# A fused decoder layer: the gated MLP in three phases, its down projection by a seven-product scheme

## The reference, cut to what matters

```python
u = rmsnorm(h, ln_ffn)
g_up, v_up = jnp.split(u @ w_up, 2, axis=-1)          # w_up: 1024 x 6144
g_up = causal_dwconv(g_up, ffn_conv_w, ffn_conv_b)    # 3 taps along the tokens
h = h + (jax.nn.gelu(g_up) * v_up) @ w_down           # w_down: 3072 x 1024
gate = jax.nn.sigmoid(rmsnorm(h, ln_ple) @ w_ple_gate)
h = h + gate * (p @ w_ple_proj)
```

## Time and profile before

| what | value |
|---|---|
| median of three runs | 646.7 us |
| profiled execution, its span | 644.5 us |
| TensorE matmul, busy | 640.1 us, 99% |
| TensorE weight load, busy | 531.3 us, 82% |
| VectorE, ScalarE, GpSimd busy | 353.6, 297.8, 325.0 us |
| HBM read | 62.74 MB, 101 GB/s over the span |

### The profile page before, as it was taken

The page is one execution under the profiler, slowest core; times in us unless marked ns, Lnnn a source line. Parts: engine busy times, 40 slices in busy tenths (PEclk is TensorE's granted clock), DMA queues, the critical chain, the costliest instruction groups (busy, mean ns, idle before and its releaser), DMA issues.

```text
span 644.5 us, 8549 instructions
## 1 busy us (share of the span) xinstructions
PE 640.1 (99%) x2925; PEld 531.3 (82%) x2925; DVE 353.6 (55%) x503; ACT 297.8 (46%) x453; POOL 325.0 (50%) x240
## 2 busy tenths in 40 slices
PE   9999999999999999999999999999999999999997
PEld 7887788888888888888888888888888888888886
DVE  4682499978659777655555555555422222222734
ACT  6779944788745454333333333333322222224420
POOL 6673443642326557555555555555555555545430
PEclk9999999999999999999999999999999999999999
DMA  8652225640403333323222232222322222222201
GB/s 314 261 159 87 85 94 139 158 120 1 165 5 127 99 98 131 98 98 98 98 98 98 98 98 97 92 92 94 106 91 94 93 96 95 97 96 99 98 34 65
DMA packets 21480, 68.69 MB, mean 107 GB/s; under 512 B 2512, under 2 KB 3152, under 8 KB 21456
## 3 DMA queue, kind: packets, MB, share of 16 engines
q1 hardware_dynamic: 21168, 68.12, 32.0%
q10 hardware_dynamic: 288, 0.27, 0.1%
HBM read 62.74 MB, written 2.10 MB: 101 GB/s over the span
## 4 chain that ended last, share of the span: by engine, by line
PE 99%; DMA 1%; DVE 0%; issue 0%
PE bank L1151 30%; PE bank L1152 30%; PE bank L1153 30%; PE bank L1347 2%; PE bank L1333 1%; PE bank L1293 1%; PE bank L1197 1%; PE bank L1200 1%; PE bank L1205 1%; DMA lead<-in_lead_in 1%; PE bank L1263 1%; PE bank L1248 0%; PE bank L1314 0%; PE bank L1190 0%; PE bank L1290 0%; DVE fin L1122 0%
## 5 line engine op out<-in xcount | busy, mean ns | idle before, releaser
L383 POOL TENSOR_TENSOR wlo<-raw,whi 128x512 fp32r<-128x512 f32 x106 | 142.7, 1346 | 260.5 <-ACT whi L444 260.1
L444 ACT ACTIVATE whi<-raw 128x1024 fp32r<-128x1024 f32 x102 | 107.5, 1057 | 213.4 <-PE bank L1153 212.8
L1151 PE MATMUL bank<-uhi,whi 128*128 128x512 f32 x488 | 189.8, 389 | 0.0
L1152 PE MATMUL bank<-ulo,whi 128*128 128x512 f32 x488 | 189.8, 389 | 0.0
L1153 PE MATMUL bank<-uhi,wlo 128*128 128x512 f32 x488 | 189.8, 389 | 0.0
L384 POOL TENSOR_TENSOR wlo<-raw,whi 128x512 fp32r<-128x512 f32 x106 | 163.1, 1539 | 0.0
L1151 PEld LDWEIGHTS bank<-uhi,whi 128*128 128x128 f32 x488 | 91.6, 188 | 19.2
L1152 PEld LDWEIGHTS bank<-ulo,whi 128*128 128x128 f32 x488 | 91.6, 188 | 19.1
L1153 PEld LDWEIGHTS bank<-uhi,wlo 128*128 128x128 f32 x488 | 91.6, 188 | 18.8
L1069 DVE SCALAR_TENSOR_TENSOR tmp<-tmp,vec 128x511 f32<-128x511 f32 (+1 forms) x48 | 64.7, 1347 | 27.7 <-ACT tmp L690 24.7
L1151 PE MATMUL bank<-acthi,whi 128*128 128x512 f32 x192 | 74.7, 389 | 0.0
(11 more groups left out here) (215 smaller groups left out, 806.0 us busy)
## 6 DMA issues: line engine op xcount, KB each, us to landing
raw<-in_weights SPq DMA_DIRECT2D x106, 512.0 KB, 3.3
res<-in_x_t SPq DMA_DIRECT2D x8, 256.0 KB, 5.6
xtok<-in_x SPq DMA_DIRECT2D x4, 512.0 KB, 8.7
raw<-in_weights SPq DMA_DIRECT2D x7, 256.0 KB, 6.6
out<-fin SPq DMA_DIRECT2D x7, 256.0 KB, 2.0
k_more<-kT SPq DMA_DIRECT2D x6, 256.0 KB, 4.9
kT<-kT SPq DMA_DIRECT2D x3, 256.0 KB, 4.2
ptok<-in_p_t SPq DMA_DIRECT2D x1, 512.0 KB, 3.4
```

The source lines that it names most:

```text
L383: nc.gpsimd.tensor_tensor(wlo[s][:, 0:CW // 2], raw[s][:, 0:CW // 2], whi[s][:, 0:CW // 2].bitcast(F32), ALU.subtract)
L444: nc.scalar.activation(whi[s][:, :], raw[s][:, :], ACT.Copy).then_inc(w_hi, 1)
L1151: mm(o, ahi, bhi, start=start, stop=False)
L1152: mm(o, ahi, blo, start=False, stop=False)
```

## The change

The hidden channels are worked through in three phases. Each phase makes 8 channel tiles (4 pairs, 16 up chunks) and at once their share of the down projection (8 down chunks), which is added to `res`. So weight chunks come in the order 16 up, 8 down, three times; `acthi` and `actlo` go and the loops over chunks are written out.

The down projection is done by Strassen's scheme on blocks of two channel tiles (a pair) x two output tiles x two token halves of 256. For each pair VectorE makes five sums of the four quarters of the activations (`pair_sums`, 1280 columns in three instructions), ScalarE the high parts (`act_pair`), VectorE the low parts (`low_plain`, `low_sums`). A down chunk holds the four quarters of a weight block as 4 x 256 columns. Of its sums, two and two are VectorE's (`weight_sums_1`, `weight_sums_2`) and one is GpSimd's (`first_sum`); ScalarE makes the high parts, 512 + 512 + 768 columns (`down_high`); GpSimd subtracts for two of the low parts (`down_low`). For the three sums in `xhi` ScalarE writes -xhi into `xlo`, and a DMA issued from GpSimd, with `accum_op=ALU.add`, adds the sums `ws` to it, 384 KB. TensorE multiplies seven products, each in a half bank of 256 columns (`down`), two chunks to each of the four output pairs. For each output pair and phase VectorE adds the four banks to `res` in six dependent instructions (`combine`).

In the last phase the norm of the last block is tied to the combines (`norm_ple`, `finish_ple`), and `p` is loaded later, into the place of two of the `ws` buffers.

```diff
-C_DN = C_UP + 2 * FT
-C_PP = C_DN + 3 * KD
+PHASES = 3
+PH_CHUNKS = 2 * FT // PHASES + KD
+PH_PAIRS = FT // PHASES // 2
+C_PP = C_UP + PHASES * PH_CHUNKS
+DOWN = [(0, 0), (1, 0), (0, 1), (1, 1), (2, 0), (2, 1), (3, 0), (3, 1)]
+B11, B22, T6, T7, T4, T3, T1 = range(7)
...
+        SETS = ((0, 1, 3, 4), (5, 6, 7, 2))
...
+                elif isinstance(c, int) and down_index(c - RING) is not None:
+                    sp.wait_ge(d_lo, 2 * (down_index(c - RING) + 1))
+                    sp.wait_ge(w_sum, 2 * (down_index(c - RING) + 1))
...
+            for c in range(C_UP, N_CHUNKS):
                 load(c, c % RING)
+                if c == C_PP + 1:
+                    sp.wait_ge(act_lo, 2 * PHASES * PH_PAIRS)
+                    sp.dma_start(ptok[:, :, :], p_t[:, :, :]).then_inc(p_in, 16)
...
+            def first_sum(n):
+                c = down_chunk(n)
+                s, quarter = c % RING, raw[c % RING][:, :].rearrange("p (b w) -> p b w", w=HALF)
+                pool.wait_ge(raw_in[s], 16 * (c // RING))
+                if n >= RING:
+                    pool.wait_ge(x_low[n % RING], 16 * (n // RING))
+                nc.gpsimd.tensor_tensor(ws[n % RING][:, 4, :], quarter[:, 2, :], quarter[:, 3, :], ALU.add).then_inc(s1_ok, 1)
...
+                pool.wait_ge(d_hi, 4 * n + 4)
+                pool.dma_start(xlo[s][:, :], ws[n % RING][:, 2:5, :].rearrange("p b w -> p (b w)"), accum_op=ALU.add).then_inc(x_low[s], 16)
...
+            def act_pair(pair):
+                act.wait_ge(f_prod, 2 * pair + 2)
+                act.wait_ge(chunk_done, C_UP + pair // PH_PAIRS * PH_CHUNKS)
+                nc.scalar.activation(ahi[:, pair % PH_PAIRS, 0:2, :], yq[:, 0:4:3, :], ACT.Copy).then_inc(act_hi, 1)
+                act.wait_ge(t_ok, 3 * (pair + 1))
+                nc.scalar.activation(ahi[:, pair % PH_PAIRS, 2:7, :], ts[:, :, :], ACT.Copy).then_inc(act_hi, 1)
+            def down_high(n):
...
+                act.wait_ge(chunk_done, c - (RING - 1))
+                nc.scalar.activation(whi[s][:, 0:CW // 2], raw[s][:, CW // 2:CW], ACT.Copy).then_inc(d_hi, 1)
+                act.wait_ge(w_sum, 2 * n + 1)
+                nc.scalar.activation(whi[s][:, CW // 2:CW], sums[:, 0:2 * HALF], ACT.Copy).then_inc(d_hi, 1)
...
+                nc.scalar.activation(xhi[s][:, :], sums[:, 2 * HALF:5 * HALF], ACT.Copy).then_inc(d_hi, 1)
+                act.wait_ge(d_hi, 4 * n + 3)
+                nc.scalar.activation(xlo[s][:, :], xhi[s][:, :].bitcast(F32), ACT.Copy, scale=-1.0).then_inc(d_hi, 1)
...
+            def norm_ple(j):
+                act.wait_ge(d_step, 6 * (4 * (PHASES - 1) + j + 1))
+                for m in (2 * j, 2 * j + 1):
+                    nc.scalar.activation(uhi[:, m, :], res[:, m, :], ACT.Copy,
+                                         scale=vec[:, V_LN_PLE + m:V_LN_PLE + m + 1]).then_inc(u_hi, 1)
+                    act.wait_ge(acc_ok, KD + m - 1)
+                    nc.scalar.activation(tmp[:, 2 + m % 2, :], res[:, m, :], ACT.Square).then_inc(sqr, 1)
...
+                for i in range(KD):
+                    high(down_chunk(ph * KD + i) + RING)
+                    if ph == PHASES - 1:
+                        if i == 3:
+                            norm_ple(0)
+                        elif i == 4:
+                            norm_ple(1)
...
+                        elif i == 6:
+                            norm_ple(2)
+                        elif i == 7:
+                            norm_ple(3)
...
+                    up_product(f + 1)
+                    pair_sums(pair)
+                    low_plain(pair)
+                weight_sums_1(n0 + 4)
+                low_sums(pair)
+                weight_sums_2(n0 + 4)
...
+                combine(4 * ph)
+                weight_sums_1(n0 + 6)
+                weight_sums_2(n0 + 6)
+                combine(4 * ph + 1)
+                weight_sums_1(n0 + 7)
+                weight_sums_2(n0 + 7)
+                if ph < PHASES - 1:
+                    combine(4 * ph + 2)
+                    combine(4 * ph + 3)
+            finish_ple(0)
+            combine(4 * ph + 2)
+            finish_ple(1)
+            dve.wait_ge(x_low[1], 16 * 2 * PHASES)
             for k in range(2):
                 dve.wait_ge(p_hi, k + 1)
                 V.tensor_tensor(pTlo[:, k, :], ptok[:, k, :], pThi[:, k, :].bitcast(F32), ALU.subtract).then_inc(p_lo, 1)
+            combine(4 * ph + 3)
+            finish_ple(2)
+            finish_ple(3)
...
+            def down(n):
+                ph, i = divmod(n, KD)
+                j, h = DOWN[i]
+                s = down_chunk(n) % RING
+                if h == 0 and j < 2:
+                    pe.wait_ge(g_out, 8 * ph + 6 + 2 * j)
+                    pe.wait_ge(v_out, 8 * ph + 6 + 2 * j)
+                elif h == 0:
+                    pe.wait_ge(d_step, 6 * (4 * ph + j - 1))
+                b0, b1, b2, b3 = SETS[j % 2]
+                products = ((2 * b2, whi, wlo, 3, T7), (2 * b2 + 1, whi, wlo, 2, T6), (2 * b0 + 1, whi, wlo, 0, T3),
+                            (2 * b1 + 1, whi, wlo, 1, T4), (2 * b0, xhi, xlo, 5, B22), (2 * b1, xhi, xlo, 4, B11),
+                            (2 * b3, xhi, xlo, 6, T1))
+                pe.wait_ge(d_lo, 2 * (n + 1))
+                pe.wait_ge(act_lo, 2 * (PH_PAIRS * ph + 2 * h + 2))
+                for at_, high, low, q, x in products:
+                    if q == 5:
+                        pe.wait_ge(x_low[s], 16 * (n // RING + 1))
+                    for k in range(2):
...
+                        last = three(cell[:, at_, :], high[s][:, w], low[s][:, w], ahi[:, 2 * h + k, x, :], alo[:, 2 * h + k, x, :],
+                                     first, h == 1 and k == 1, True)
+                last.then_inc(chunk_done, 1)
```

More of the change, by code:

```diff
@@ new lines, in _ @@
+            for ph in range(PHASES):
+                for p in range(PH_PAIRS):
+                    pair = ph * PH_PAIRS + p
+                    f, c = 2 * pair, up_chunk(2 * pair, 0)
+                    if pair:
+                        high(c + RING)
+                    tap_up(f)
+                    if pair:
+                        high(c + RING + 1)
+                    gelu_up(f)
+                    high(c + RING + (2 if pair else 3))
+                    tap_up(f + 1)
+                    if pair and p < PH_PAIRS - 1:
+                        high(c + RING + 3)
+                    gelu_up(f + 1)
+                    if p == PH_PAIRS - 1:
+                        high(c + RING + 3)
+                    act_pair(pair)
+                for i in range(KD):
+                    high(down_chunk(ph * KD + i) + RING)
[4 more added lines that the diff above has]
+                            norm_ple(1)
+                        elif i == 5:
+                            act.wait_ge(p_in, 16)
+                            act.wait_ge(x_low[0], 16 * 2 * PHASES)
+                            act.wait_ge(d_lo, 2 * (PHASES * KD - 3))
+                            for k in range(2):
+                                nc.scalar.activation(pThi[:, k, :], ptok[:, k, :], ACT.Copy).then_inc(p_hi, 1)
+                        elif i == 6:
+                            norm_ple(2)
+                        elif i == 7:
+                            norm_ple(3)
@@ new lines, in up_product, with pair_sums @@
+            def up_product(f):
+                g, y = tmp[:, f % 2, :], tmp[:, 2 + f % 2, :]
+                dve.wait_ge(v_out, f + 1)
+                dve.wait_ge(f_gelu, f + 1)
+                V.tensor_tensor(y, g, y, ALU.mult).then_inc(f_prod, 1)
+            def pair_sums(pair):
+                dve.wait_ge(f_prod, 2 * pair + 2)
+                if pair:
+                    dve.wait_ge(act_lo, 2 * pair)
+                V.tensor_tensor(ts[:, 0:2, :], yq[:, 0:4:2, :], yq[:, 1:4:2, :], ALU.add).then_inc(t_ok, 1)
+                V.tensor_tensor(ts[:, 2:4, :], yq[:, 0:2, :], yq[:, 2:4, :], ALU.subtract).then_inc(t_ok, 1)
+                V.tensor_tensor(ts[:, 4, :], yq[:, 0, :], yq[:, 3, :], ALU.add).then_inc(t_ok, 1)
@@ new lines, in finish_ple @@
+            def finish_ple(j):
+                for m in (2 * j, 2 * j + 1):
+                    dve.wait_ge(u_hi, 2 * KD + m + 1)
+                    V.scalar_tensor_tensor(ulo[:, m, :], res[:, m, :], vec[:, V_LN_PLE + m:V_LN_PLE + m + 1],
+                                           uhi[:, m, :].bitcast(F32), ALU.mult, ALU.subtract).then_inc(u_lo, 1)
+                    dve.wait_ge(sqr, KD + m + 1)
+                    dve.wait_ge(acc_ok, KD + m)
+                    V.tensor_tensor(acc[:, :], acc[:, :], tmp[:, 2 + m % 2, :], ALU.add).then_inc(acc_ok, 1)
@@ L1438, in _, with up_pair @@
                 channels(C_UP + 4 + s, s, mbank[4 + s][:, :], uhi, ulo, 0, KD, True, True)
-            with pe.Fori(2, FT // 2) as it:
+            def up_pair(pair):
+                ph, p = divmod(pair, PH_PAIRS)
                 for t in range(2):
                     for half in range(2):
```

(21 more changed lines are left out.)

277 lines of the change are left out of this document (175 added, 102 removed).

## The result

The changed kernel takes 658.5 us (657.9 to 658.8) against 647.1 us (646.3 to 648.9): a ratio of 1.0168, 95% interval 1.0146 to 1.0190. It is slower by 11.4 us where 4.8 us less was forecast, and lies outside the range of 637.5 to 651.0.

A forecast was written before the change was run, and what follows sets the result against it. TensorE was taken to bound the kernel: -10.5 us of matmuls, +5.0 tail, +0.6 combine cover and +0.1 end of the up part make -4.8, so 641.9 us, range 637.5 to 651.

The forecast's parts named there:

- What bounds the kernel: Whole kernel: TensorE, busy 640.1 of 644.5 us, so only matmul time or a new TensorE stall moves the end.
- The matmul term: Down projection: 1008 matmuls of 256 columns at 119.1 ns replace 576 at 226.7 ns, 10.5 us less.
- the estimate of 14: Down projection: the saving in us if matmul steps followed the skill page's stated gap, 215.8 and 109.2 ns.
- The combine's cover of 0.4 us: Down part: combine(0) ends at 19.6, TensorE needs its banks at 20.0; 0.2 us per phase taken, 0.6 in all.
- The adding transfer: Down chunks: GpSimd's DMA lands 6 us after issue, about 1 on GpSimd; costs nothing below 9.7 us.
- The fourth rival: Down chunks: the adding transfer delays TensorE's fifth product; slower than before from 11.3 us on, 654.8 at 14; chance 0.13.
- The end of the up part: VectorE's chain behind the last up matmul takes 7 to 9.5 us of 10.0; 0.1 us taken, bounds 0 to 12.
- The contention: Up part: VectorE and GpSimd together fill 21.2 of 21.8 us per pair of channel tiles, nearly full but enough.
- The tail: Last phase: TensorE waits for pTlo, then pp, behind the combines and norms; 5.0 us of stall, bounds 3.3 to 9.
- the third: Rival, end of the up part: VectorE late by 1 to 4 us in each phase, 645 to 654; chance 0.22.

The follow-up runs named there:

- e1_order: Changed kernel with only the order at each up part's end altered: last pair's taps and sums first on ScalarE and VectorE; 661.2 us, ratio 1.0221.
- e9_order_tail: e7_apart_order_tail without any of GpSimd's waits for its own instructions, so the reorderings and the moved channel sum alone; 657.9 us, ratio 1.0171.
- e4_pool_lows: Changed kernel with the adding transfer undone: GpSimd subtracts all five low parts of a down chunk itself; 673.2 us, ratio 1.0411.
- e11_one_pause: e7_apart_order_tail with only one of GpSimd's waits for itself kept, behind the first sum after each adding transfer's issue; 641.5 us, ratio 0.9908.
- e13_small_transfer: e4_pool_lows plus an unused 8 KB transfer issued by GpSimd behind each subtraction of the three sums; 676.7 us.
- e2_tail: Changed kernel with only the tail reordered: pTlo ahead of finish_ple(1) on VectorE, keep_pp ahead of norm_ple(3) on ScalarE; 661.5 us, ratio 1.0232.
- e6_apart_order: Changed kernel with the order of e1_order and GpSimd waiting for the end of each of its own MLP instructions; 649.3 us, ratio 1.0033.
- e7_apart_order_tail: e6_apart_order plus the tail order of e2_tail, with the channel sum moved from the second gate chunk to the third; 645.0 us, ratio 0.9964.

## Why the prediction was wrong

- **What bounds the kernel**: right. All but 0.7 us of the result is TensorE's matmuls, its waits, its clock or the late start.
- **The matmul term** (119.1 ns, -10.5): right. Measured 120.0, -9.6; the estimate of 14 from the Trainium skill (TensorE: Matmul & The Clock Gate, Back-to-back issue gap) was not reached.
- **The combine's cover of 0.4 us** (+0.6): harmless in the kernel after, with no wait there, but it is where e1_order and e9_order_tail lost 4.3 to 5.4 us in each phase.
- **The adding transfer** (6 us to landing, about 1 on GpSimd, hidden below 9.7): right as a price, 5.8 and 0.9. The fourth rival did not occur. That its issue would change VectorE's turns was in no term.
- **The end of the up part** ("Cover 0.5 to 3 us", taken at 0.1 us): **this step failed.** It let VectorE's chain begin at the last up matmul and last 7 to 9.5 us; it ended after 15.5 (283.52 to 298.98), and after 13.8 in the other phases. Its links were near their prices, 8.4 us together (the pair sums 3.6 where 1.6 to 3 was given); what the forecast left out was that the value tile is read 7 us late (5.3 in the other phases), behind a tap that waits on ScalarE behind `high()` and behind two weight sums. The working had noticed the same lateness in the kernel before and ScalarE's `high()` calls, and still took 0.1 of its own bounds 0 to 12. The measured 10.9 us of idle time lies near their upper end. e1_order, which moves just these instructions, reads the value tile after 2.0, 0.5 and 0.5 us, and both stalls go.
- **The contention** ("nearly full, still enough", and a rest of 1.29 that makes 0.69 at most 1.98): wrong in kind. A sum of busy times assumes that VectorE gets its turn after one GpSimd instruction. Without a DMA issue of GpSimd it does (e4_pool_lows); with one, e1_order shows 0.68 become 8.20. The earlier trace rows could not tell: the kernel before has no such issue. The Trainium skill (SBUF — State Buffer, Who interferes with whom) says that an instruction of VectorE with two SBUF inputs contends with GpSimd's reads, and for VectorE's 2-port modes that the first to issue has the shared ports for its whole instruction. The trace agrees that the one blocks the other, but the bound of one instruction that the forecast drew from it does not hold: the wait spanned seven.
- **The tail** (+5.0): the mechanism was right, `pTlo` and then `pp`. The idle was 2.9 us, below the bounds of 3.3 to 9, and 1.6 us of half clock behind it make 4.5.
- **The clock**: no term at all, 4.6 us measured. The kernel before has no gap between matmuls from the up part on, and full granted clock all the way.
- **The rivals**: the third happened, at 0.22, but was priced at 1 to 4 us a phase. It took 3.5 to 3.8 of idle a phase, and 1.5 of half clock on top in two of them: 5 us, above that price. The range of 651 stopped short of even the priced 654, since it was cut where one in ten was left.

With these stalls removed the forecast's size does appear, 641.5 measured against 641.9, but by luck: the profile of e11_one_pause has no stall in the tail and instead 2.7 us of waits for the adding transfer and 1.6 of half clock.

**Left open**: by what mechanism a DMA issue changes who gets the turn, and what ends the lock-out; why the gap of 2.7 us at 430.19 was not followed by half clock and that at 561.25 was; and why the up part starts up to 2.6 us later in some profiles. How much of the 10.9 us is order and how much lock-out has no single answer, since the two are not additive: the order alone brought the last low sums 6.0 to 6.5 us forward, leaving out GpSimd's low parts 2.8 to 4.4, the pauses alone 1.2 to 1.5.

## What to carry to other kernels

Where VectorE and GpSimd work side by side on SBUF, don't add up their busy times: look for GpSimd's DMA issues, and put a gap behind the first instruction that follows each, since a VectorE instruction with two SBUF inputs may else wait through all that GpSimd has lined up; one pause of 0.08 us in each down chunk was worth 16 us here (e9_order_tail against e11_one_pause). Follow the chain behind the last matmul of a stage through each engine's written order, with all that stands ahead of each link, and where its price reaches from 0 to 12 us don't take 0.1. When a fix gives nothing, read what became late instead before giving it up: neither the orders nor the pauses alone reached the time of the kernel before, together they beat it.

## What the runs showed of the hardware

- Beside back-to-back GpSimd arithmetic (e4_pool_lows) VectorE's two-input instructions took turns, 2.3 us at most for 512 elements. Behind a DMA issue of GpSimd, be it of 384 KB or of 8 KB, one of 0.68 us lasted up to 8.20 (6.31 with the small one), to GpSimd's next gap or, in some cases, its next issue.
- Behind every gap of 2.9 us or more (the longest 8.3, e13_small_transfer), and behind part of those of 2.0 to 2.7 us, TensorE worked at half clock for 3.3 to 6.0 us and lost 1.3 to 2.7 us each time, starting up to 1.6 us after it had resumed (e2_tail). Behind gaps of 2.7 us (430.19 in the kernel after) and 2.8 us (570.88 in e6_apart_order), among others, it did not.
- The adding transfer of 384 KB between tiles in SBUF landed after 5.8 us (4.8 in e7_apart_order_tail, where the issue waits for GpSimd's instruction before it) and took 0.9 us of GpSimd, against 1.98 us for the subtraction that it replaces.
